# Four edits at the seams between the stages of a two-layer encoder trunk: a shorter wait, a split in halves, another order on VectorE and GpSimd, and other load times

## The chip, the cores and the metric

The kernel runs on one core of a Trainium2 chip. The metric is the device time of one execution in microseconds (us), the median of several executions.

## The reference

A trunk of two layers over 1024 tokens of width 1024, batch 1, all in float32. What is computed, cut to the matrices:

```python
cond = silu(c)
for i in range(2):
    shift1, scale1, gate1, shift2, scale2, gate2 = split(cond @ mod_w[i] + mod_b[i], 6)
    h = rms_norm(x, norm1_gain[i]) * (1 + scale1) + shift1
    if i == 0:
        y = swa_sink_attention(h, ...)        # q, k, v of width 1024, 128, 128; window of 128 keys; @ w_o
    else:
        uv = gelu(h @ w_uv)                   # 1024 x 4096
        u, v = split(uv, 2)
        v = layer_norm(v, v_gain)
        s = einsum('gij,bnjgc->bnigc', masked(w_s), blocks(v)) + s_bias
        y = (u * s) @ w_o                     # 2048 x 1024
    x = x + gate1 * y
    h = rms_norm(x, norm2_gain[i]) * (1 + scale2) + shift2
    x = x + gate2 * (square(relu(h @ w1)) @ w2)     # 1024 x 4096, 4096 x 1024
```

## The kernel before

**Numbers.** Each float32 product is made of three matmuls: both operands are split into a high part (an `ACT.Copy` into fp32r on ScalarE, `split_hi` and `weight_high`) and a low part (source minus high part, on GpSimd or VectorE), and high x high, low x high and high x low are added up in PSUM. A weight block is 1024 x 128 (`w_raw`, `w_hi`, `w_lo`, two slots of 128 x 1024).

**Three products in the fast form.** `fast_mlp(L)` runs three times: for the MLP of layer 0 (L.layer 0), for the gated stage of layer 1 (1, `L.gated`), for the MLP of layer 1 (2). The first product (up) has 16 pairs of output blocks. Pairs 0 and 1 are *plain*: 8 k-steps of 3 matmuls for each of two blocks and two halves of the tokens. The other 14 (n = 0 to 13 in the code, output pair j = n + 2) are Strassen-like: 7 products (t = 0 to 6) of 12 matmuls of 128 x 512 each. The second product (down) follows with pairs n = 14 and up, in couples that alternate on TensorE: (14, t), (15, t), (14, t + 1) and so on. A combination of weight quarters (`S_1` to `S_4`, GpSimd, line 853) is the weight of products 1 to 4. Its low part is made on GpSimd for t < 3 (line 858) and on VectorE for t >= 3 (line 1831).

**Outputs of the first product.** For each pair the ReLU and square of four blocks (B12, B22, B11, B21; `squared`, line 1836) and four differences of them (T3, T1, T2, T4; `output_diff`, line 1840) are made on VectorE and stored to `hid_dram` by SyncE's queue, one DMA each (line 642). The second product reads them back by operand, four pairs in one load of 1 MB on ScalarE's queue (`load_operand`, line 1143); then `operand_high` (ScalarE, 128 x 2048, line 1139) and `operand_low` (VectorE, 128 x 2048, line 1825).

**SyncE's queue is a fixed list.** At the start of `load_fast` the order is: the four plain blocks, the quarters of n = 0, `save_pair(0)`, `load_early(1)` (A11 and A21 of n = 1), `save_pair(1)`, and only then, in the loop, `load_a12(1)`, `load_a22(1)`, `load_early(2)`, `save_pair(2)`. `save_pair(j)` waits for each of the seven blocks of pair j in turn; the last is T4. The change does not touch this list. `S_1` of a pair needs its A21 and A22, `S_2` needs `S_1`, and the low part of product t = 1 follows `S_2` in GpSimd's list.

**The end of a stage.** Layers 0 and 1 of `fast_mlp` keep the last four output pairs' operands for a plain `closing` (TensorE line 2212, matmuls counted under line 2180): 4 pairs of blocks on the first half of the tokens, then 4 on the second. Its units alternate between the PSUM tiles pp[0] and pp[1]. The last couple before it writes pp[0] and pp[2] (first of the couple) and pp[3] and pp[2] (second). VectorE adds each down product to x (line 1935, counter `x_ev`).

**The start of a stage.** `opening_pair` runs plain pair 0 into pp[3] and pp[0] while VectorE and ScalarE normalise; then `plain_unit` twice. The weight split of plain pair 1, block 0, needs slot 0, which pair 0, block 0 frees three k-steps before TensorE has finished pair 0. VectorE's list there: `combine_inputs` (lines 1800 to 1817), the outputs of pair 0, `operand_low` of inputs 1, 2, 4, 6, two weight lows, the outputs of pair 1, then `up_step(0)`. ScalarE copies product t = 2 of n = 0 into a tile (line 1340) that the ReLU of pair 1 uses, so it waits for the last square of pair 1 (`u_quad`), and TensorE's t = 4 waits for that copy.

Of the kernel before, what the change touches and what calls it, by code (L numbers as in the profile page):

```python
# [15 lines left out]
KC = D // P  # L16
HALF = 512
# [80 lines left out]
def build(nc, x_in, c_in, pos_in, weights, mod_w, cols, mats, ws_in, bias_in, q_dram, v_dram, out):  # L98
# [5 lines left out]
    with ctx:  # L104
# [125 lines left out]
        v_pad = sem("v_pad")  # L230
        quad_in = [sem(f"quad_in{i}") for i in range(QUADS)]
# [119 lines left out]
        class Layer:  # L351
# [430 lines left out]
        def _(pool):  # L782
# [25 lines left out]
            def fast_weights(L):  # L808
# [94 lines left out]
        def _(act):  # L903
# [215 lines left out]
            def fast_mlp(L):  # L1119
# [166 lines left out]
                first = L.first  # L1286
                act.wait_ge(gemm, 2 * first + 1)
                split_hi(first + 1, 0)
# [38 lines left out]
                for p in range(PRODUCTS * L.pairs):  # L1327
# [13 lines left out]
                    if last and t % 2 == 0:  # L1341
# [70 lines left out]
        def _(dve):  # L1412
# [382 lines left out]
            def fast_mlp(L):  # L1795
# [59 lines left out]
                def plain_outputs(j, tiles, by):  # L1855

                    if j:
                        dve.wait_ge(hid_out, L.stored(j))
# [3 lines left out]
                    squared(j, O_B11, tiles[0][:, 0:HALF], by[0][:, 0:HALF])  # L1862
                    dve.wait_ge(u_quad, L.quad(j, 2))
                    output_diff(j, O_T3, O_B22, O_B12)
                    late_diffs(j)
                    squared(j, O_B21, tiles[1][:, 0:HALF], by[1][:, 0:HALF])
                    last_diff(j)

                def up_step(n):
# [10 lines left out]
                    for t in range(POOL_LOWS + (2 if n == 0 else 0), PRODUCTS):  # L1880
                        weight_low(n, t)
                    dve.wait_ge(f_copy, L.threes + 3 * n + 3)
                    add(3, banks[1], banks[1], 2)
                    if last:
# [3 lines left out]
                        operand_low(1)  # L1888
                        return
# [3 lines left out]
                    add(4, copied[1], banks[0], 1)  # L1893
# [33 lines left out]
                def down_step(n, t):  # L1927
# [12 lines left out]
                    if L.couple(n) == 0:  # L1940
                        if L.second(n) and t < 5:
                            operand_low(t + 2)
# [179 lines left out]
                else:  # L2122
                    plain_outputs(0, (pp[3], pp[0]), (tmp[:, 0, :], tmp[:, 1, :]))
                operand_low(1)
                dve.wait_ge(t_sum, L.sums + 13)
                operand_low(2)
                if L.gated:
                    stats(2)
                    stats(3)
                for t in (4, 6):  # L2130
                    operand_low(t)
# [518 lines left out]
```

## Time and profile before

| | us |
|---|---|
| median of 3 runs (lowest 2188.77, highest 2193.66) | 2189.37 |
| the profiled execution's own time | 2189.19 |
| its span in the profile | 2187.4 |
| TensorE matmuls busy | 2112.1 (97%) |
| VectorE busy | 1515.4 (69%) |
| ScalarE busy | 934.7 (43%) |
| GpSimd busy | 946.5 (43%) |

The profile's span runs from the first to the last instruction; 1.8 us lie around it. "Idle before" is the time an engine stood still ahead of an instruction, with the engine and line that released it. PEclk or "granted clock" is the share of TensorE's full clock: 1.00 is 2.4 GHz and 0.50 is 1.2 GHz.

### The profile page before, as it was taken

How to read it: one execution, taken by the hardware profiler on the slowest of the kernel's cores; microseconds unless marked ns; L12 is line 12 of the kernel's file. 1: busy time of each engine (PE TensorE's matmuls, PEld its weight loads, DVE VectorE, ACT ScalarE, POOL GpSimd, SP SyncE). 2: the span in 40 equal slices, each digit the busy share in tenths (PEclk: the TensorE clock that was granted, in tenths of full speed). 3: DMA queues.
4: the chain of work that ended last, by engine and by line, in shares of the span. 5: the costliest groups of instructions: out<-in, count | busy, mean ns of one | idle time of the engine just before them, and what ended most of it. 6: DMA issues, size and time to landing. Idle time of an engine off the chain costs nothing. (4 is left out here: it accounts for less than half of the span.)

```text
span 2187.4 us, 27285 instructions
## 1 busy us (share of the span) xinstructions
PE 2112.1 (97%) x9700; PEld 1714.5 (78%) x9700; DVE 1515.4 (69%) x1775; ACT 934.7 (43%) x1453; POOL 946.5 (43%) x600
## 2 busy tenths in 40 slices
PE   6999999999999999999899999999999999999999
PEld 4886687788887888787777788778778888778887
DVE  8679689766537878567787554756786666865673
ACT  4337543433344442334444666533343434443341
POOL 0124412555547466312443333622165555664753
PEclk8999999999999999999999999999999999999999
DMA  7363532444445664331665455633244444655352
GB/s 273 117 182 97 204 114 73 158 155 154 145 164 166 214 230 157 98 96 61 191 211 184 153 183 173 190 127 95 68 145 154 159 155 172 212 178 172 98 180 90
DMA packets 188896, 336.30 MB, mean 154 GB/s; under 512 B 32737, under 2 KB 55137, under 8 KB 188258
## 3 DMA queue, kind: packets, MB, share of 16 engines
q1 hardware_dynamic: 130018, 216.15, 29.8%
q10 hardware_dynamic: 58752, 118.50, 16.1%
q8 instruction: 75, 1.23, 0.2%
q14 instruction: 51, 0.42, 0.1%
HBM read 249.65 MB, written 83.89 MB: 152 GB/s over the span
## 5 line engine op out<-in xcount | busy, mean ns | idle before, releaser
L2541 PE MATMUL pp<-hid_lo,w_hi 128*128 128x512 f32 x1184 | 468.8, 396 | 16.6 <-POOL w_lo L858 8.4
L2541 PE MATMUL pp<-hid_lo,w_lo 128*128 128x512 f32 x1184 | 462.7, 391 | 0.0
L2541 PE MATMUL pp<-hid_hi,w_hi 128*128 128x512 f32 x1184 | 462.5, 391 | 0.0
L1133 ACT ACTIVATE w_hi<-mod_t 128x512 fp32r<-128x512 f32 x296 | 186.7, 631 | 426.8 <-POOL mod_t L853 225.8
L2541 PE MATMUL pp<-h_hi,w_hi 128*128 128x512 f32 x888 | 349.2, 393 | 2.6 <-issue 2.6
L2541 PE MATMUL pp<-h_hi,w_lo 128*128 128x512 f32 x888 | 346.2, 390 | 0.0
L2541 PE MATMUL pp<-h_lo,w_hi 128*128 128x512 f32 x888 | 346.2, 390 | 0.0
L785 POOL TENSOR_TENSOR w_lo<-w_raw,w_hi 128x1024 fp32r<-128x1024 f32 x44 | 112.6, 2560 | 479.1 <-ACT w_hi L908 479.1
L2180 PE MATMUL pp<-h_hi,w_hi 128*128 128x512 f32 x736 | 274.8, 402 | 24.0 <-POOL w_lo L785 10.0
L858 POOL TENSOR_TENSOR w_lo<-w_raw,w_hi 128x512 fp32r<-128x512 f32 x58 | 84.4, 1455 | 466.6 <-ACT w_hi L1133 420.0
L2541 PEld LDWEIGHTS pp<-hid_lo,w_hi 128*128 128x128 f32 x1184 | 223.6, 189 | 70.7 <-POOL w_lo L858 14.5
L2180 PE MATMUL pp<-h_lo,w_hi 128*128 128x512 f32 x736 | 268.9, 394 | 0.0
L2180 PE MATMUL pp<-h_hi,w_lo 128*128 128x512 f32 x736 | 268.8, 394 | 0.0
L1935 DVE SCALAR_TENSOR_TENSOR x<-pp,mod,x 128x512 f32<-128x512 f32 x224 | 166.6, 746 | 141.8 <-PE pp L2541 141.6
L2541 PEld LDWEIGHTS pp<-hid_lo,w_lo 128*128 128x128 f32 x1184 | 223.1, 188 | 47.7
L2541 PEld LDWEIGHTS pp<-hid_hi,w_hi 128*128 128x128 f32 x1184 | 223.6, 189 | 44.5
L858 POOL TENSOR_TENSOR w_lo<-mod_t,w_hi 128x512 fp32r<-128x512 f32 x148 | 239.1, 1615 | 13.4 <-ACT w_hi L1133 13.4
L853 POOL TENSOR_TENSOR mod_t<-w_raw 128x512 f32<-128x512 f32 x116 | 159.3, 1373 | 191.6 <-DVE w_lo L1831 161.4
L2541 PEld LDWEIGHTS pp<-h_hi,w_hi 128*128 128x128 f32 x888 | 167.2, 188 | 37.8 <-issue 4.0
L2541 PEld LDWEIGHTS pp<-h_hi,w_lo 128*128 128x128 f32 x888 | 167.0, 188 | 35.3
L2541 PEld LDWEIGHTS pp<-h_lo,w_hi 128*128 128x128 f32 x888 | 167.2, 188 | 33.6
L2180 PEld LDWEIGHTS pp<-h_hi,w_hi 128*128 128x128 f32 x736 | 138.5, 191 | 61.9 <-issue 13.1
(227 smaller groups left out, 3186.5 us busy)
## 6 DMA issues: line engine op xcount, KB each, us to landing
wide_f<-hid_dram ACTq DMA_DIRECT2D x64, 1024.0 KB, 5.8
hid_dram<-wide_f SPq DMA_DIRECT2D x247, 256.0 KB, 3.1
w_raw<-weights SPq DMA_DIRECT2D x232, 256.0 KB, 3.1
w_raw<-weights SPq DMA_DIRECT2D x70, 512.0 KB, 3.5
wide_f<-weights SPq DMA_DIRECT2D x64, 256.0 KB, 4.5
wide_f<-mod_w ACTq DMA_DIRECT2D x48, 256.0 KB, 3.9
mod_first<-mod_w SPq DMA_DIRECT2D x16, 512.0 KB, 15.3
mod_t<-mod_w ACTq DMA_DIRECT2D x16, 512.0 KB, 4.4
```

Of the source, the lines that this page charges most:

```text
L785: nc.gpsimd.tensor_tensor(out=w_lo[:, s, :, :], in0=w_raw[:, s, :, :], in1=w_hi[:, s, :, :].bitcast(f32), op=ALU.subtract).then_inc(lo_don ...
L853: nc.gpsimd.tensor_tensor(out=out, in0=in0, in1=in1, op=op).then_inc(w_sum, 1)
L858: nc.gpsimd.tensor_tensor(out=L.weight_quad(w_lo, n, t), in0=L.weight_source(n, t), in1=L.weight_quad(w_hi, n, t).bitcast(f32), op=ALU.sub ...
L1133: nc.scalar.activation(L.weight_quad(w_hi, n, t), L.weight_source(n, t), ACT.Copy).then_inc(w_high, 1)
L1935: V.scalar_tensor_tensor(out=xn, in0=L.product_banks(n)[BANK[t]], scalar=mod[:, L.gate, 2 * q + m:2 * q + m + 1], in1=xn, op0=ALU.mult, op ...
L2180: last = T.matmul((pp[s] if tile is None else tile)[:, cs], w[:, s, order[k] if order else k, :], r[:, k, cs], start=(k == 0 and w is w_hi ...
L2541: last = T.matmul(bank, w[:, i, :], r[:, i, :], start=(t in FRESH and i == 0 and w is high and r is hi), stop=(i == QUADS - 1 and w is low ...
```

## The change

Four places of `fast_mlp` and its neighbours:

1. TensorE's wait ahead of `closing` asks for the last update of the first pair of the last couple, not of the second. In `closing` the first unit runs its 8 k-steps in a row and then the second unit; before, the eighth k-step of the first came after four of the second.
2. Plain pair 1, block 0: ScalarE and GpSimd split the block in two halves of 4 k-steps (128 x 512), with two new semaphores, and TensorE starts after the first half.
3. VectorE's list at the start of the two ungated stages (`plain_start`): all four squares of a pair come before its differences; `operand_low(6)` and the differences of pair 1 come later (T3 after all weight lows of n = 0; T1, T2, T4 in `up_step(0)` behind the sum of product t = 4).
4. First operands of the second product: `load_operand(0, t)` is issued at every product t = 0 to 6 of the last up pair (before: 0 to 3 at t = 0, 2, 4, 6 and 4 to 6 in the first down pair); the high part of operand 2 and its low part move ahead of the down product; in the first couple GpSimd makes `S_1` and `S_2` of the first pair before the low part of the second pair's product 0.

```diff
             def sums_done(self, n, r):
+                if self.couple(n) == 0 and r in (S_1, S_2):
+                    return 4 * (self.pairs_before + FAST_UP) + 2 * self.second(n) + (1 if r == S_1 else 2)
 # GpSimd, fast_weights
-                for pair in range(1, PLAIN_PAIRS):
-                    for s in range(2):
-                        split_lo(L.first + pair, s)
+                pool.wait_ge(half_high, L.layer + 1)
+                second_low(0).then_inc(half_low, 1)
+                pool.wait_ge(hi_done, 2 * L.first + 3)
+                second_low(1).then_inc(lo_done, 1)
+                split_lo(L.first + 1, 1)
...
-                    for n in (first, first + 1):
-                        weight_low(n, 0)
-                        if c:
-                            sum_of(n, S_1)
-                    if c == 0:
-                        sum_of(first, S_1)
-                        sum_of(first + 1, S_1)
-                    for r, t in ((S_2, 1), (S_4, 2)):
-                        for n in (first, first + 1):
-                            sum_of(n, r)
-                            weight_low(n, t)
+                    weight_low(first, 0)
+                    sum_of(first, S_1)
+                    if c == 0:
+                        sum_of(first, S_2)
+                    weight_low(first + 1, 0)
+                    sum_of(first + 1, S_1)
+                    if c:
+                        sum_of(first, S_2)
+                    weight_low(first, 1)
+                    sum_of(first + 1, S_2)
+                    weight_low(first + 1, 1)
+                    for n in (first, first + 1):
+                        sum_of(n, S_4)
+                        weight_low(n, 2)
 # ScalarE
-                split_hi(first + 1, 0)
+                for part, counter in ((0, half_high), (1, hi_done)):
+                    ks = slice(QUADS * part, QUADS * part + QUADS)
+                    nc.scalar.activation(w_hi[:, 0, ks, :], w_raw[:, 0, ks, :], ACT.Copy).then_inc(counter, 1)
...
-                    if last and t % 2 == 0:
+                    if last:
                         act.wait_ge(f_mm, L.mms + p + 1)
                         if t == 0:
                             act.wait_ge(hid_out, L.stored(L.first_out + QUADS))
-                        load_operand(0, t // 2)
-                    if n == FAST_UP and t < 3:
-                        load_operand(0, t + 4)
+                        load_operand(0, t)
...
-                    if last and t in (3, 5):
-                        group_operand(0, t // 2 - 1)
-                    if n == FAST_UP and t < 5:
-                        group_operand(0, t + 2)
+                    if last and 3 <= t < 6:
+                        group_operand(0, t - 3)
+                    if n == FAST_UP and t < 4:
+                        group_operand(0, t + 3)
 # VectorE
+                def plain_start():
+                    plain_squares(0, (pp[3], pp[0]), (tmp[:, 0, :], tmp[:, 1, :]))
+                    plain_diffs(0)
+                    operand_low(1)
+                    dve.wait_ge(t_sum, L.sums + 13)
+                    operand_low(2)
+                    operand_low(4)
+                    weight_low(0, 3)
+                    dve.wait_ge(hid_out, L.stored(1))
+                    plain_squares(1, (pp[1], pp[2]), (tmp[:, 0, :], mod_acc[:, :]))
+                    weight_low(0, 4)
+                    weight_low(0, 5)
+                    weight_low(0, 6)
+                    dve.wait_ge(u_quad, L.quad(1, 2))
+                    output_diff(1, O_T3, O_B22, O_B12)
+                    operand_low(6)
...
+                    if n == 0:                      # up_step, behind add(3, ...)
+                        add(4, copied[1], banks[0], 1)
+                        late_diffs(1)
+                        last_diff(1)
...
 # TensorE
-                    for k in range(KC - 1):
+                    for k in range(KC):
                         if k % QUADS == 0:
                             pe.wait_ge(op_low, quads + k // QUADS)
-                        products(0, k, hi, lo, (0,), order=order)
-                    ready(pair0, 1)
-                    for k in range(4):
-                        products(1, k, hi, lo, (0,), order=order)
-                    products(0, KC - 1, hi, lo, (0,), order=order).then_inc(gemm, 1)
-                    for k in range(4, KC):
-                        last = products(1, k, hi, lo, (0,), order=order)
+                        last = products(0, k, hi, lo, (0,), order=order)
                     last.then_inc(gemm, 1)
+                    unit(pair0, 1, hi, lo, halves=(0,), order=order)
...
-            pe.wait_ge(x_ev, fast[0].updates(fast[0].pairs - 1, 6))
+            pe.wait_ge(x_ev, fast[0].updates(fast[0].pairs - 2, 6))
             closing(fast[0].first + PLAIN_PAIRS, h_hi, h_lo, 2, quads=fast[0].lows_ready(DOWN_GROUPS[0], 0))
             fast_mlp(fast[1])
-            pe.wait_ge(x_ev, fast[1].updates(fast[1].pairs - 1, 6))
+            pe.wait_ge(x_ev, fast[1].updates(fast[1].pairs - 2, 6))
```

## Rows read from the trace of the kernel before

**Rows 1.** The page: busy time of each engine, share of the span, instructions.
```profile
PE 2112.1 (97%) x9700; PEld 1714.5 (78%) x9700; DVE 1515.4 (69%) x1775; ACT 934.7 (43%) x1453; POOL 946.5 (43%) x600
```

**Rows 2.** Waits of TensorE, whole span: total us, times, longest.
```profile
PE pp L2180 <- POOL w_lo L785: 10.0, 7, 3.2
```

**Rows 3.** Timeline of TensorE, first closing: start, us, [idle before].
```profile
894.52 0.50 PE L2180 MATMUL pp<-h_hi,w_hi 128*128 128x512 f32 x1 [2.28 <-DVE x L1935]
908.23 0.50 PE L2180 MATMUL pp<-h_hi,w_hi 128*128 128x512 f32 x1 [0.88 <-POOL w_lo L785]
```

**Rows 4.** Timelines of VectorE and GpSimd, first closing.
```profile
891.51 2.29 DVE L1970 TENSOR_TENSOR h_lo<-wide_f,h_hi 128x2048 fp32r<-128x2048 f32 x1 [0.75 <-ACT h_hi L1157]
...
895.17 5.23 DVE L1970 TENSOR_TENSOR h_lo<-wide_f,h_hi 128x2048 fp32r<-128x2048 f32 x2 [0.70 <-ACT h_hi L1157]
...
905.80 2.37 POOL L785 TENSOR_TENSOR w_lo<-w_raw,w_hi 128x1024 fp32r<-128x1024 f32 x1 [9.75 <-ACT w_hi L908]
```

**Rows 5.** Stretches: TensorE, its loads, VectorE, ScalarE, GpSimd busy; clock; DMA.
```profile
361.00:366.00 5.00, 5.00 (x12) 3.86 (x13) 5.00 (x6) 0.48 (x1) 2.39 (x1) 0.50 0.56 197
896.00:899.00 3.00, 3.00 (x9) 2.32 (x8) 3.00 (x2) 0.94 (x1) 0.06 (x1) 0.51 0.48 164
1613.00:1619.00 6.00, 5.68 (x24) 4.43 (x24) 3.15 (x6) 1.58 (x3) 1.28 (x1) 1.00 0.73 237
```

**Rows 6.** Timelines, start of the first MLP.
```profile
355.00 1.06 ACT L908 ACTIVATE w_hi<-w_raw 128x1024 fp32r<-128x1024 f32 x1 [2.30 <-PE pp L2180]
...
360.76 1.19 PE L2180 MATMUL pp<-h_hi,w_hi 128*128 128x512 f32 x2 [3.17 <-POOL w_lo L785]
...
379.50 3.72 ACT L1139 ACTIVATE hid_lo<-wide_f 128x2048 fp32r<-128x2048 f32 x2 [0.44 <-DMA hid_dram<-wide_f]
...
391.62 0.50 PE L2541 MATMUL pp<-hid_lo,w_hi 128*128 128x512 f32 x1 [0.71 <-POOL w_lo L858]
397.88 0.47 PE L2541 MATMUL pp<-hid_lo,w_hi 128*128 128x512 f32 x1 [0.53 <-ACT tmp L1340]
```

**Rows 7.** Timelines, from the last difference of pair 1 to product (1, 1), first MLP.
```profile
397.08 0.69 DVE L1840 TENSOR_TENSOR wide_f<-wide_f 128x512 f32<-128x512 f32 x1
398.49 0.42 SPq L593 DMA_DIRECT2D w_raw<-weights  x1
402.47 1.64 POOL L853 TENSOR_TENSOR mod_t<-w_raw 128x512 f32<-128x512 f32 x1 [2.31 <-issue]
405.78 1.30 POOL L858 TENSOR_TENSOR w_lo<-mod_t,w_hi 128x512 fp32r<-128x512 f32 x1
408.88 0.39 PE L2541 MATMUL pp<-hid_lo,w_hi 128*128 128x512 f32 x1
```

**Rows 8.** Timeline of TensorE, start of the gated stage and of the third.
```profile
1013.18 0.70 PE L2180 MATMUL pp<-h_hi,w_hi 128*128 128x512 f32 x2 [1.43 <-POOL w_lo L785]
...
1613.08 0.47 PE L2541 MATMUL pp<-hid_lo,w_hi 128*128 128x512 f32 x1 [2.67 <-ACT tmp L1340]
1624.60 0.39 PE L2541 MATMUL pp<-hid_lo,w_hi 128*128 128x512 f32 x1
```

**Rows 9.** Timelines, first couple of the first MLP's second product.
```profile
651.71 0.63 ACT L1133 ACTIVATE w_hi<-wide_f 128x512 fp32r<-128x512 f32 x1 [3.50 <-DMA wide_f<-weights]
652.42 1.28 POOL L858 TENSOR_TENSOR w_lo<-wide_f,w_hi 128x512 fp32r<-128x512 f32 x1 [4.63 <-ACT w_hi L1133]
...
660.99 0.47 PE L2541 MATMUL pp<-hid_lo,w_hi 128*128 128x512 f32 x1 [1.71 <-DVE hid_hi L1825]
663.21 3.34 POOL L853 TENSOR_TENSOR mod_t<-w_raw,mod_t 128x512 f32<-128x512 f32 x1
667.84 0.50 PE L2541 MATMUL pp<-hid_lo,w_hi 128*128 128x512 f32 x1 [1.12 <-POOL w_lo L858]
674.71 0.47 PE L2541 MATMUL pp<-h_hi,w_hi 128*128 128x512 f32 x1 [0.88 <-issue]
```

**Rows 10.** The page, DMA issues: count, KB each, median us from issue to landing.
```profile
wide_f<-hid_dram ACTq DMA_DIRECT2D x64, 1024.0 KB, 5.8
```

More of the change, by code:

```diff
@@ L230, in build @@
         v_pad = sem("v_pad")
+        half_high, half_low = sem("half_high"), sem("half_low")
         quad_in = [sem(f"quad_in{i}") for i in range(QUADS)]
@@ L859, in weight_low, with second_low @@
                                             in1=L.weight_quad(w_hi, n, t).bitcast(f32), op=ALU.subtract).then_inc(w_low_p, 1)
-                for pair in range(1, PLAIN_PAIRS):
-                    for s in range(2):
-                        split_lo(L.first + pair, s)
+                def second_low(part):
+                    ks = slice(QUADS * part, QUADS * part + QUADS)
+                    return nc.gpsimd.tensor_tensor(out=w_lo[:, 0, ks, :], in0=w_raw[:, 0, ks, :],
+                                                   in1=w_hi[:, 0, ks, :].bitcast(f32), op=ALU.subtract)
+                pool.wait_ge(half_high, L.layer + 1)
[3 more added lines that the diff above has]
+                split_lo(L.first + 1, 1)
                 for n in range(FAST_UP):
@@ L1286, in fast_mlp @@
                 first = L.first
+                act.wait_ge(raw_in[0], 16 * (first + 1) + 16)
                 act.wait_ge(gemm, 2 * first + 1)
-                split_hi(first + 1, 0)
+                for part, counter in ((0, half_high), (1, hi_done)):
+                    ks = slice(QUADS * part, QUADS * part + QUADS)
+                    nc.scalar.activation(w_hi[:, 0, ks, :], w_raw[:, 0, ks, :], ACT.Copy).then_inc(counter, 1)
                 if L.gated:
@@ L1853, in last_diff, with plain_squares @@
                     output_diff(j, O_T4, O_B21, O_T2)
-                def plain_outputs(j, tiles, by):
-                    if j:
-                        dve.wait_ge(hid_out, L.stored(j))
+                def plain_squares(j, tiles, by):
                     dve.wait_ge(f_relu, L.relus + 2 * j + 2)
@@ L1862, in plain_outputs, with plain_diffs @@
                     squared(j, O_B11, tiles[0][:, 0:HALF], by[0][:, 0:HALF])
+                    squared(j, O_B21, tiles[1][:, 0:HALF], by[1][:, 0:HALF])
+                def plain_diffs(j):
                     dve.wait_ge(u_quad, L.quad(j, 2))
@@ L1865, in plain_outputs @@
                     late_diffs(j)
-                    squared(j, O_B21, tiles[1][:, 0:HALF], by[1][:, 0:HALF])
                     last_diff(j)
+                def plain_start():
[14 more added lines that the diff above has]
+                    operand_low(6)
                 def up_step(n):
@@ L1879, in up_step @@
                     last = n == FAST_UP - 1
-                    for t in range(POOL_LOWS + (2 if n == 0 else 0), PRODUCTS):
-                        weight_low(n, t)
+                    if n:
+                        for t in range(POOL_LOWS, PRODUCTS):
+                            weight_low(n, t)
                     dve.wait_ge(f_copy, L.threes + 3 * n + 3)
@@ L1888, in up_step @@
                         operand_low(1)
+                        operand_low(2)
                         return
+                    if n == 0:
+                        add(4, copied[1], banks[0], 1)
+                        late_diffs(1)
+                        last_diff(1)
                     dve.wait_ge(hid_out, L.stored(j))
@@ L1892, in up_step @@
                     squared(j, O_B12, banks[1], rectified[0])
-                    add(4, copied[1], banks[0], 1)
+                    if n:
+                        add(4, copied[1], banks[0], 1)
                     dve.wait_ge(f_sum, L.threes + 3 * n + 2)
@@ L1940, in down_step @@
                     if L.couple(n) == 0:
-                        if L.second(n) and t < 5:
-                            operand_low(t + 2)
+                        if L.second(n) and t < 4:
+                            operand_low(t + 3)
                         if not L.gated and not L.second(n) and 1 <= t <= 4:
@@ L2121, in fast_mlp @@
                     stats(1)
[L2122 to L2127, printed above, removed]
+                    operand_low(1)
+                    dve.wait_ge(t_sum, L.sums + 13)
+                    operand_low(2)
                     stats(2)
                     stats(3)
-                for t in (4, 6):
-                    operand_low(t)
-                weight_low(0, 3)
-                weight_low(0, 4)
-                if not L.gated:
-                    plain_outputs(1, (pp[1], pp[2]), (tmp[:, 0, :], mod_acc[:, :]))
+                    for t in (4, 6):
+                        operand_low(t)
+                    weight_low(0, 3)
+                    weight_low(0, 4)
+                else:
+                    plain_start()
                 if L.closes:
@@ L2150, in fast_mlp @@
                     gate_slot(FAST_UP, 0)
+                    operand_low(2)
                 for p in range(PRODUCTS * FAST_UP, PRODUCTS * L.pairs):
@@ L2488, in plain_unit @@
                 def plain_unit(pair, s, tile, turns=()):
-                    pe.wait_ge(lo_done, 2 * pair + s + 1)
+                    if s == 0:
+                        pe.wait_ge(half_low, L.layer + 1)
+                    else:
+                        pe.wait_ge(lo_done, 2 * pair + s + 1)
                     for k in range(KC):
+                        if (s, k) == (0, QUADS):
+                            pe.wait_ge(lo_done, 2 * pair + 1)
                         last = products(s, k, h_hi, h_lo, tile=tile)
```

## The prediction, on record before the changed kernel was run

> **What bounds the kernel.** First the page: TensorE's matmuls are busy 97% of the span [rows 1], so time can only come out of its idle gaps or of its slow clock. Then the list of who TensorE waited for: the largest release is the low half of plain weights, 10.0 us in 7 waits [rows 2]. Then TensorE's timeline, to see where each gap lies; and the table of stretches, because a gap can cost twice. In rows 5 the granted clock is 0.50 (1.2 GHz) for five microseconds after the 3.17 us gap of [rows 6], and 0.51 in the stretch behind the 2.28 us gap of a closing, while no drop follows the 2.67 us gap of the third stage [rows 5, 8]. Last, the timelines of the other engines around each gap, to see what becomes late when the gap closes. The four products of 12 matmuls between 397.88 and 408.88 [rows 6, 7] take 11.0 us with one restart in them; I count 2.72 us for an unhindered product, 10.9 us for 48 matmuls, 21.8 us for the 96 of two plain blocks.
>
> **Part 1, the closings (two of them).** TensorE stands 2.28 us, until VectorE has made the last update, which stands in its list behind a 128 x 2048 subtraction that ends at 893.80 [rows 3, 4]. The first unit writes pp[0]; the second pair of the couple used pp[3], so the shorter wait is already met when TensorE arrives at 894.52 - 2.28 = 892.24. The next waits: k-step 4 needs that subtraction (893.80) at 892.24 + 2.72 = 894.96, met. 48 matmuls then end at 903.1. The next unit began at 908.23 after 0.88 us of idle, because `gemm` of the first unit came late (its last k-step was put after four others) and ScalarE's 1.06 us and GpSimd's 2.37 us follow it [rows 3, 4, 6]. With the new order `gemm` comes at 897.7, the low half is ready by 898.9, or, since VectorE's two subtractions hold GpSimd up until 900.40 [rows 4], by 902.8. VectorE must still clear a tile and make one update behind 900.40, about 903.3. So the unit starts at about 903.3 instead of 908.23: 4.9 us, of which 2.28 and 0.88 are idle and the rest is the slow clock that followed the gap. Bounds: 4.0 if that update waits for GpSimd's low, 5.1 if nothing does. The second closing shows the same gaps of 2.28 and 0.88. Two closings: 9.8 us.
>
> **Part 2, halves.** At the start of the first MLP the halves of ScalarE (about 0.6 us for 128 x 512, from half of 1.06) and GpSimd (1.30, [rows 7]) end at about 357.1, before TensorE has finished pair 0 at 360.76 - 3.17 = 357.59 [rows 6]. The idle of 3.17 goes, and with it the stretch at 0.50: between 361 and 366 it cost half of 5 us, 2.5 us. In the gated stage the gap is 1.43 [rows 8], in the third the same within 0.02, without a drop. The second half has 5.4 us of cover (4 k-steps of 6 matmuls). ScalarE and GpSimd pay one more instruction each, hidden. So TensorE comes to product (0, 0) earlier by 5.7, 1.4 and 1.4 us. What that is worth is read from what follows.
>
> **Part 3, squares first, in stages 0 and 2.** At the start of the first MLP the gaps 0.71 and 0.53 remain [rows 6], in the third 2.67 [rows 8]. The order removes the 2.67 (ScalarE's copy then waits for four squares of pair 1, not for three differences and `operand_low(6)` too). But two things come late. First, ScalarE: its two high parts of 3.72 us in all can't start before the stores of pair 0 have landed (379.50, [rows 6]); behind them lie 1.0 for a ReLU, two weight highs of 0.63, 1.0 for a ReLU and 0.6 for the copy, 387.1 to 387.8. So product (0, 2), for which TensorE is there at 357.6 + 21.8 + 2 x 2.72 = 384.8, starts at about 387.9, (0, 4) at 393.3. Second, SyncE's list. T4 of pair 1 is now made behind the sum of product t = 4. Not before 393.3 + 2.8 (the product) + 0.7 (the sum) + 2.0 (three differences at 0.69) = 398.8, I take 399.2; before it ended at 397.77 [rows 7]. `load_a22(1)` stands behind it in SyncE's list. From T4's end to the end of the low part of (1, 1) the trace has 407.08 - 397.77 = 9.3 us, made of the store's issue, the loads, their landing (GpSimd stood until 402.47), two sums and the low part [rows 7]. So (1, 1) starts at about 408.6 and not, as free running would have it, at 357.6 + 21.8 + 8 x 2.72 = 401.1. Before it was 408.88 [rows 7]: all of the 5.7 + 0.71 + 0.53 us come back as one idle of about 4.4 us, 0.3 are left. And an idle of that size is longer than the 3.17 that brought the slow clock, so I take 2.3 us for that (between the 1.7 of a closing and 2.5). If the 3.1 us ahead of (0, 2) brings a drop too, 2.5 more; I count 0.5 of it. First MLP: 0.3 - 2.3 - 0.5 = -2.5 us, a loss. Bounds: -6 and +7.8 (free running).
> Third stage, the same working: (0, 2) at 1603.8, (0, 4) at 1609.2, T4 at 1615.7, + 9.4 = 1625.1 against 1624.60 [rows 8]: -0.5, and -2.3 for the clock: -2.8 us. Bounds -6 and +4.6. The gated stage has its own list, without this order; I keep 1.0 of its 1.43.
>
> **Part 4, the second product.** At its start stand 1.71, 1.12 and 0.88 us in the first MLP [rows 9], the same three within 0.04 in the third stage; the gated one has only two such gaps, 2.1 in all. The operands come one product earlier each, so the 1.71 and the 0.88 go. The 1.12 is GpSimd's chain: nine instructions from 652.42 to 667.8, where TensorE is released. Two now come earlier, so seven remain behind 652.5, each 1.3, and each held for 2.05 us more when it meets a 128 x 2048 subtraction (3.34 against 1.30, [rows 9, 7]). With two held the low part that (14, 2) needs comes at 666.1, TensorE is there at 664.7. Of 4.9 (the three gaps, a smaller one of about 0.3 between them and restarts) I take off 1.4 there and 0.7 for what this pushes: 2.8 us each for the first and third, and 1.3 for the gated one: 6.9 us. Bounds per stage 0 and 4.9 (all gaps).
> The Trainium skill, SBUF — State Buffer, "Who interferes with whom", says that a VectorE instruction with two SBUF inputs and a GpSimd one that reads SBUF exclude each other for a whole instruction. The 3.34 against 1.30 agrees. By that rule the third early subtraction (operand 2) holds GpSimd a third time, 668.1 instead of 666.1, no gain at (14, 2), and the sum for this part would be 3.9 and not 6.9. I keep two, because ScalarE's highs space the subtractions out.
>
> **Sum.** 9.8 - 2.5 - 2.8 + 1.0 + 6.9 = 12.4 us from 2189.19 (the profiled execution's time; the median of the runs is 0.18 above), 2176.8; I say 2177.
>
> **Rivals.** (a) *All gaps close:* T4 of pair 1 does not hold the reload, or holds it behind other cover. Speaks for it: VectorE has its weight lows out of the way. Against: SyncE's list [rows 7]. Gain 9.8 + 7.8 + 4.6 + 1.4 + up to 6.9 = 30, 2159 to 2165. (b) *The stage starts lose less:* the later idle brings no slow clock, as after the 2.67, or the reload lands sooner: 4 to 9 us better than my sum, 2167 to 2172. (c) *The early loads crowd:* seven loads of 1 MB in seven products are 385 GB/s, where a load that takes 5.8 us [rows 10] had two products to itself; part 4's gain is lost and the stage starts stay: 2183 to 2188, near no change. (d) *Slower:* the same crowding at the same place makes the weights of pair 15 late. Before, ScalarE waited for them until 651.71 [rows 9]; with a high of 0.63 and a low of 1.28 behind it, and TensorE there at 661 - 1.7 - 2.7 = 656.6, they may be 3 us later before TensorE stands. Behind that each us costs one, and from about 3 us of idle 2.6 more by clock. It decides from landings near 658: 3 x (2.3 + 3 + 2.6) = 24 us against a sum of 12.4, about 2200.
>
> **Chances.** Forecast 0.54, (a) 0.12, (b) 0.16, (c) 0.13, (d) 0.05. The forecast's own range is 2172 to 2183; with (b) and most of (c) 2167 to 2185, which leaves out (a), (d) and the edges. A change of 0.2%, 4.4 us, is about what a measurement of this kernel can tell from none. Faster by more 0.84, within 0.11, slower 0.05.
>
> **What would show it.** Right: no idle ahead of the closings' first matmul, clock 1.00 there; no idle at the first plain block of pair 1; a new gap of 4 us or more before product (1, 1) of the first and third stage, released by GpSimd, whose sum waits for a DMA, and clock 0.50 behind it; (14, 2) idle about 1 us. Wrong: no such gap, or the loads of w_raw issued before T4, or a gap ahead of (15, 0).

## The result, and the profile after

The changed kernel takes 2195.04 us (median of 8 runs, 2192.53 to 2196.72); the kernel before, beside it, 2190.66 (8 runs). The ratio is 1.0025, 95% interval 1.0015 to 1.0035: slower by 4.4 us in the medians and 5.5 by the ratio, where 12.4 us faster were forecast. The profiled execution of after took 2192.53 us (span 2190.7), against 2189.19 before: +3.3 us.

The two closings did what they should, and something else lost more than both gave. To find it I lay the matmuls of the fast products of the two traces side by side (6216 in each, in the same order) and take how much later each product starts in the changed kernel. The difference of that shift over a stretch is what the stretch lost (+) or won. "Couple" is the first couple of the second product, pairs 14 and 15. The halves of the first MLP lie in the first row, those of the two other stages in the closing rows: product (0, 0) is the first one behind them.

| stretch | forecast | measured in after |
|---|---|---|
| first MLP, up to product (2, 0) | +2.5 | +3.7 |
| first MLP, couple | -2.8 | +1.5 |
| closing 1, and halves of the gated stage | -4.9 - 1.0 | -7.0 |
| gated stage, couple | -1.3 | **+8.1** |
| closing 2, and halves of the third stage | -4.9 - 1.4 | -7.0 |
| third stage, (0, 0) to (2, 0) | +4.2 | +3.6 |
| third stage, couple | -2.8 | +0.8 |
| all the rest | 0 | -0.3 |

A closing alone is 5.3 (experiment 1), so 1.7 of each closing row are halves. The third stage's start, halves included, is 3.6 - 1.7 = +1.9, against 4.2 - 1.4 = +2.8 forecast.

Timeline of TensorE after (start, us, instruction, [idle before <- releaser]), the gaps that answer to [rows 6 to 9], and the one of the gated stage:
```profile
389.21 0.47 PE L2580 MATMUL pp<-hid_lo,w_hi 128*128 128x512 f32 x1 [3.91 <-ACT tmp L1357]
410.84 0.76 PE L2580 MATMUL pp<-hid_lo,w_hi 128*128 128x512 f32 x1 [3.43 <-POOL w_lo L861]
664.93 0.50 PE L2580 MATMUL pp<-hid_lo,w_hi 128*128 128x512 f32 x1 [1.52 <-POOL w_lo L861]
669.46 0.50 PE L2580 MATMUL pp<-hid_lo,w_hi 128*128 128x512 f32 x1 [1.51 <-POOL w_lo L861]
673.98 0.50 PE L2580 MATMUL pp<-hid_lo,w_hi 128*128 128x512 f32 x1 [1.51 <-POOL w_lo L861]
1382.11 2.08 PE L2519 MATMUL pp<-ws,mod_acc 128*128 128x128 f32 x8 [7.71 <-ACT mod_acc L1243]
```
Gone are the 3.17 us ahead of pair 1, and the 2.28 and 0.88 of the closings. New are 3.91 and 3.43 in the first MLP, and 1.95 and 3.51 at the same two places of the third stage. In the first MLP's couple, 1.71 + 1.12 + 0.88 became three times 1.5. And in the gated stage, behind the last product of its last up pair, TensorE stands for 7.7 us, at a place where the kernel before had no gap at all.

The stretches around them (us of the stretch, then busy us and count of TensorE, its weight loads, VectorE, ScalarE, GpSimd; granted clock; DMA share; GB/s): one behind the 3.43, one at the closing, then the gated stage:
```profile
411.00:413.00 2.00, 2.00 (x5) 1.62 (x6) 1.93 (x3) 0.94 (x2) 2.00 (x2) 0.50 0.91 329
896.00:900.00 4.00, 4.00 (x19) 3.34 (x18) 2.97 (x3) 3.20 (x3) 1.33 (x1) 1.00 0.13 52
...
1360.00:1365.00 5.00, 5.00 (x31) 4.40 (x30) 1.83 (x3) 1.96 (x6) 0.00 (x0) 1.00 1.02 389
1365.00:1370.00 5.00, 5.00 (x25) 4.17 (x25) 2.95 (x5) 4.40 (x7) 1.30 (x1) 1.00 1.08 358
1370.00:1375.00 5.00, 4.40 (x24) 3.46 (x22) 1.72 (x1) 0.00 (x0) 2.58 (x2) 1.00 1.07 363
1375.00:1380.00 5.00, 0.00 (x0) 0.00 (x0) 0.00 (x0) 0.63 (x2) 0.00 (x0) 0.69 1.06 323
1380.00:1385.00 5.00, 2.89 (x11) 2.70 (x12) 2.41 (x3) 5.00 (x8) 3.04 (x3) 0.50 0.83 284
```
At the closing the clock stays at 1.00 (in [rows 5] it was 0.51 there). In the gated stage a stretch comes in which no engine does anything to speak of while the DMA engines are full: TensorE 0.00, VectorE 0.00, ScalarE 0.63, GpSimd 0.00, DMA share 1.06 at 323 GB/s. The whole core waits for the weights of pair 15. ScalarE's and SyncE's timelines name it:
```profile
1355.46 0.40 ACTq L1157 DMA_DIRECT2D wide_f<-hid_dram  x1
...
1358.12 0.38 ACTq L1157 DMA_DIRECT2D wide_f<-hid_dram  x1
...
1360.85 0.37 ACTq L1157 DMA_DIRECT2D wide_f<-hid_dram  x1
...
1364.46 0.37 ACTq L1157 DMA_DIRECT2D wide_f<-hid_dram  x1
...
1368.09 0.37 ACTq L1157 DMA_DIRECT2D wide_f<-hid_dram  x1
1379.37 0.63 ACT L1147 ACTIVATE w_hi<-wide_f 128x512 fp32r<-128x512 f32 x1 [9.97 <-DMA wide_f<-weights]
...
1380.42 1.63 ACT L1243 ACTIVATE mod_acc<-mod_acc,vscale 128x128 f32<-128x128 f32 x4
```
```profile
1363.31 8.18 SPq L596 DMA_DIRECT2D wide_f<-weights  x4
```
Five loads of 1 MB are issued in 12.6 us. Behind the third of them SyncE comes to its four weight loads of pair 15 (256 KB each), and takes 8.18 us for their issue alone; the next two of 1 MB fall beside it. The list of DMA issues in this stretch gives their time to landing (KB each, median us):
```profile
wide_f<-hid_dram ACTq DMA_DIRECT2D x7, 1024.0 KB, 9.9
hid_dram<-wide_f SPq DMA_DIRECT2D x8, 256.0 KB, 5.1
w_raw<-weights SPq DMA_DIRECT2D x5, 256.0 KB, 3.4
wide_f<-weights SPq DMA_DIRECT2D x4, 256.0 KB, 14.0
```
14.0 us for the weights; in the same stretch of the kernel before it is 6.4. ScalarE stands 9.97 us for the first high part of pair 15. Queued behind that in ScalarE's list is the scaling of the gated stage's normalised v (`v_dram`), L1243, at 1380.42, and it is this that TensorE's matmuls at 1382.11 wait for: not for pair 15's weights themselves. Behind the gap the granted clock is 0.50 (1.2 GHz), and TensorE's matmuls take 0.63 us instead of 0.39 until some 1387.

### The profile page after: what moved, and what is told of

It reads as the page before. It is cut to its first block and busy times, and to the rows that moved or that the text cites. A ratio compares the mean times of both kernels' runs of the same rounds, so it can differ in the third digit from the quotient of the medians.

```text
span 2190.7 us, 27291 instructions
## 1 busy us (share of the span) xinstructions
PE 2109.8 (96%) x9700; PEld 1714.5 (78%) x9700; DVE 1508.7 (69%) x1775; ACT 934.6 (43%) x1456; POOL 943.1 (43%) x603
## 5 line engine op out<-in xcount | busy, mean ns | idle before, releaser
L861 POOL TENSOR_TENSOR w_lo<-mod_t,w_hi 128x512 fp32r<-128x512 f32 x148 | 234.5, 1584 | 27.1 <-ACT w_hi L1147 27.1
L788 POOL TENSOR_TENSOR w_lo<-w_raw,w_hi 128x1024 fp32r<-128x1024 f32 x41 | 107.2, 2616 | 268.5 <-ACT w_hi L922 268.4
L2580 PEld LDWEIGHTS pp<-h_hi,w_hi 128*128 128x128 f32 x888 | 167.3, 188 | 35.6 <-DVE w_lo L1846 0.7
L1147 ACT ACTIVATE w_hi<-w_raw 128x512 fp32r<-128x512 f32 x174 | 109.3, 628 | 155.6 <-PE pp L2580 145.8
```

Of the source, the lines that this page charges most:

```text
L788: nc.gpsimd.tensor_tensor(out=w_lo[:, s, :, :], in0=w_raw[:, s, :, :], in1=w_hi[:, s, :, :].bitcast(f32), op=ALU.subtract).then_inc(lo_don ...
L861: nc.gpsimd.tensor_tensor(out=L.weight_quad(w_lo, n, t), in0=L.weight_source(n, t), in1=L.weight_quad(w_hi, n, t).bitcast(f32), op=ALU.sub ...
L1147: nc.scalar.activation(L.weight_quad(w_hi, n, t), L.weight_source(n, t), ACT.Copy).then_inc(w_high, 1)
L2580: last = T.matmul(bank, w[:, i, :], r[:, i, :], start=(t in FRESH and i == 0 and w is high and r is hi), stop=(i == QUADS - 1 and w is low ...
```

## The experiments

Ten kernels. Times are against the runs of the kernel before taken beside them (medians 2189.2 to 2190.0; beside the changed kernel it was 2190.66, so a difference from the changed kernel may be 1 us off). Kernels 9 and 10 ran on another chip than 1 to 8, each beside the kernel before. The table at the end of this section has their stretches.

**1. The closings alone.** The kernel before, with this part of the change:
```diff
-                    for k in range(KC - 1):
+                    for k in range(KC):
...
-                    products(0, KC - 1, hi, lo, (0,), order=order).then_inc(gemm, 1)
...
+                    unit(pair0, 1, hi, lo, halves=(0,), order=order)
...
-            pe.wait_ge(x_ev, fast[0].updates(fast[0].pairs - 1, 6))
+            pe.wait_ge(x_ev, fast[0].updates(fast[0].pairs - 2, 6))
```


> The kernel before with the closings' part alone. The two closings in the changed kernel's trace each took back 5.2 to 5.5 us. If that gain belongs to the closings, this kernel is 10 to 11 us faster than before (ratio 0.995). If part of it was only the recovery of time that the changed kernel had lost just ahead of them, it is 8 us or less.

Measured: 2179.08 us (5 runs), ratio 0.9954 (0.9942 to 0.9967), 10 us faster. Each closing gives 5.3 us here, as in the changed kernel. The gain is theirs, and it is there whatever stands ahead. The stretches of this kernel, at the first closing:
```profile
890.00:894.00 4.00, 4.00 (x20) 3.30 (x19) 3.25 (x3) 3.20 (x3) 1.00 (x1) 1.00 0.17 67
894.00:898.00 4.00, 4.00 (x19) 3.31 (x18) 3.29 (x3) 3.23 (x3) 1.66 (x1) 1.00 0.24 70
```
TensorE is busy throughout at clock 1.00: the gaps of [rows 3] and the slow stretch of [rows 5] are gone together.

**2. The changed kernel without part 4.** Loads, high and low parts of the second product's operands and GpSimd's list are those of before; the rest is the change.

> The changed kernel with part 4 undone (loads, high and low parts of the second product's operands and GpSimd's list as before). Theory: part 4 cost about 10 us, nearly all in the gated stage, where the weights of pair 15 landed 6.5 us later behind early loads of 1 MB; so this kernel is 5 to 9 us faster than before, about 10 faster than the changed one, and has no idle near 7 us ahead of the last pair of the gated stage. Rival: the loss comes from the starts of the stages (halves and squares), and part 4 is near nothing: then it stays within 3 us of the changed kernel.

Measured: 2185.32 us (11 runs), 0.9981 (0.9972 to 0.9990): 4 us faster than before, 9.7 below the changed kernel. The 7.7 us are gone, and the gated couple costs 1.3 instead of 8.1. The gain against before is a little below the 5 to 9 expected, and why is not shown: the trace is of this kernel's slowest execution (2188.38), which has +6.5 at the third stage's start where the changed kernel, with the same code there, had +3.6.

**3. Only the loads as before.** All is as in the changed kernel but the place of the seven issues:
```diff
-                    if last:
+                    if last and t % 2 == 0:
...
-                        load_operand(0, t)
+                        load_operand(0, t // 2)
+                    if n == FAST_UP and t < 3:
+                        load_operand(0, t + 4)
```


> The changed kernel in which only the issue of the second product's seven 1 MB loads is as before (every second product of the last pair, the last three in the next pair); the order of highs, subtractions and GpSimd's list is the new one. Theory, early loads crowd SyncE's four 256 KB weight loads: the weights of pair 15 land some 6 us earlier in the gated stage, its 7.7 us idle goes, the time is 8 to 10 us below the changed kernel's. Rival, the new order of GpSimd's and VectorE's lists costs it: 2 us or less below the changed kernel's.

Measured: 2185.75 us (12 runs), 0.9984 (0.9975 to 0.9993), 9.3 below the changed kernel. This separates the transfers from the order of the lists: the order is still the new one, and the loss of the gated couple is 0.6 (the trace is of the fastest execution, 2181.59). The weights of pair 15 land in 7.3 us and not in 14.0. The same list of issues, of this kernel:
```profile
wide_f<-hid_dram ACTq DMA_DIRECT2D x7, 1024.0 KB, 7.2
...
wide_f<-weights SPq DMA_DIRECT2D x4, 256.0 KB, 7.3
```
ScalarE's wait for them (timeline) falls from 9.97 to 2.26 us:
```profile
1367.32 0.63 ACT L1147 ACTIVATE w_hi<-wide_f 128x512 fp32r<-128x512 f32 x1 [2.26 <-DMA wide_f<-weights]
```
In the first and third stage the couple costs 0.1 and -0.1: with the old loads the new order of high parts, subtractions and sums is worth nothing; the 6.9 us forecast had counted on order and early loads together. The gaps only move. In the first MLP one of 2.51 us, again behind GpSimd's low part, takes the place of the three:
```profile
665.80 0.50 PE L2582 MATMUL pp<-hid_lo,w_hi 128*128 128x512 f32 x1 [2.51 <-POOL w_lo L861]
```

**4. The reload ahead of the last stores.** The changed kernel, in which SyncE issues the reload of two quarters after three stores of pair 1 (B22, T3, B11) and not after all seven:
```diff
-                    save_pair(1)
+                    save_pair(1, slice(0, 3))
+                    load_a12(1)
+                    load_a22(1)
+                    save_pair(1, slice(3, None))
                 for n in range(FAST_UP):
-                    load_a12(n + 1)
-                    load_a22(n + 1)
+                    if n or L.gated:
+                        load_a12(n + 1)
+                        load_a22(n + 1)
```


> The changed kernel, but in the first MLP and the third stage SyncE issues the reload of A12 and A22 ahead of the last four stores of pair 1 (T1, T2, B21, T4). Theory, the reload stands behind T4: the 3.43 and 3.51 us idle ahead of product (1, 1) and the slow clock behind go, 4 to 9 us below the changed kernel's time. Rival, the reload is not what (1, 1) waits for, or its cover goes at once to the next wait (ScalarE's copies, the last differences): less than 2 us below, with the idle moved to (1, 2) or later.

Measured: 2186.72 us (11 runs), 0.9986 (0.9977 to 0.9995), 8.3 below the changed kernel. The start of the first MLP costs -0.1 instead of +3.7, that of the third stage 0.0 instead of +3.6. SyncE's timeline shows why, the reload at 396.54 where after had it at 402.74:
```profile
396.01 0.43 SPq L645 DMA_DIRECT2D hid_dram<-wide_f  x1
396.54 0.89 SPq L596 DMA_DIRECT2D w_raw<-weights  x2
400.23 2.74 SPq L645 DMA_DIRECT2D hid_dram<-wide_f  x4
```
The cover behind it is thin: one product later TensorE stands again, for ScalarE's copy, as the rival had it, only for less than half as long:
```profile
411.40 0.47 PE L2584 MATMUL pp<-hid_lo,w_hi 128*128 128x512 f32 x1 [1.64 <-ACT tmp L1361]
```

**5. Three loads early, four late.** The changed kernel; loads 0, 1 and 2 stay early, 3 goes behind product 6, 4 to 6 into the next pair:
```diff
-                    if last:
+                    if last and t in (0, 1, 2, 6):
...
-                        load_operand(0, t)
+                        load_operand(0, min(t, 3))
+                    if n == FAST_UP and t < 3:
+                        load_operand(0, t + 4)
```


> The changed kernel, with loads 0, 1 and 2 of the second product's operands issued early, behind products 0, 1 and 2 of the last pair; load 3 behind its product 6 and loads 4 to 6 in the next pair, both as in the kernel before. Theory, bytes crowd: the four 256 KB weight loads of pair 15 go out near products 4 and 5, now free of 1 MB loads, so the gated stage's 7.7 us idle goes: 6 to 9 us below the changed kernel's time. Rival, any early load behind product 1 delays the last stores or the chain behind them: less than 3 us below.

Measured: 2187.50 us (12 runs), 0.9994 (0.9983 to 1.0004), 7.5 below the changed kernel. The gated couple costs 1.5, the weights land in 8.7 us. So it is not that an early load delays things as such: the two loads (3 and 4) issued at 1364 and 1368, beside the weights, decide (load 3 goes out at 1375 here, 4 to 6 later still). The same stretches as above, in this kernel:
```profile
1365.00:1370.00 5.00, 5.00 (x28) 4.29 (x27) 2.92 (x5) 4.57 (x7) 1.30 (x1) 1.00 1.08 363
1370.00:1375.00 5.00, 4.97 (x26) 3.91 (x25) 2.54 (x2) 1.68 (x4) 3.03 (x3) 1.00 1.11 292
```
The DMA share reaches 1.11, as full as in the changed kernel, and TensorE is still busy in 5.00 and 4.97 of 5 us: a full row of DMA engines says nothing by itself. What counts is how many bytes share the engines with those that are waited for.

**6. The squares alone.** The kernel before with part 3 alone.

> The kernel before with part 3 alone (squares ahead of differences, T4 of pair 1 behind the sum of product 4), in the first MLP and the third stage. Theory: T4 of pair 1 comes later, the reload behind it in SyncE's list as well, and (1, 1) waits: 2 to 6 us slower than before (each stage loses 1 to 3). Rival: without the halves TensorE comes 1.7 to 5.7 us later to (0, 0), so T4 is in time and the gaps of 0.71, 0.53 and 2.67 close: 2 to 4 us faster.

Measured: 2193.97 us (12 runs), 1.0022 (1.0012 to 1.0031), 4.7 slower. The two starts lose 4.0 and 2.6 us, 6.6 together. TensorE stands ahead of (1, 1) in both, though it comes there without the halves' 5.7 us:
```profile
410.65 0.79 PE L2563 MATMUL pp<-hid_lo,w_hi 128*128 128x512 f32 x1 [4.25 <-POOL w_lo L858]
...
1626.09 0.50 PE L2563 MATMUL pp<-hid_lo,w_hi 128*128 128x512 f32 x1 [3.77 <-POOL w_lo L858]
```

**7. Closings and halves.** The kernel before with parts 1 and 2. The halves are this (TensorE's side):
```diff
-                    pe.wait_ge(lo_done, 2 * pair + s + 1)
+                    if s == 0:
+                        pe.wait_ge(half_low, L.layer + 1)
+                    else:
+                        pe.wait_ge(lo_done, 2 * pair + s + 1)
                     for k in range(KC):
+                        if (s, k) == (0, QUADS):
+                            pe.wait_ge(lo_done, 2 * pair + 1)
```


> The kernel before with the closings and the halves. The closings alone gave 10 us. Theory, the time won ahead of (0, 0) in the first MLP and the third stage is given back at the next waits (stores, ScalarE's copies, reload), and only the gated stage keeps its 1.7: 11 to 13 us faster than before. Rival, the halves are worth their idle and clock in all three stages (5.7 + 1.7 + 1.7): 17 to 19 us faster.

Measured: 2177.57 us (6 runs), 0.9938 (0.9921 to 0.9955), 11.7 us faster than before by the medians and 13.6 by the ratio, and with kernel 8 the fastest of all; that it beats kernel 1 is likely but inside the intervals. In the first MLP the 6.0 us won ahead of (0, 0) come back at (0, 2), where ScalarE's copies and GpSimd's low part stand behind the stores of pair 0:
```profile
389.84 0.80 PE L2553 MATMUL pp<-hid_lo,w_hi 128*128 128x512 f32 x1 [4.63 <-POOL w_lo L859]
```

**8. All but part 4, with the reload first.** The kernel before with closings, halves and squares, and the edit of kernel 4.

> The kernel before with closings, halves and squares, and the reload of A12 and A22 ahead of the last four stores of pair 1; part 4 left out. If part 4 (10 us) and the place of the reload (8 us) add, it is 16 to 20 below the changed kernel's time, 11 to 15 faster than before. If both took back the same time twice, it is no more than 12 below the changed kernel's, 7 faster than before.

Measured: 2177.47 us (5 runs), 0.9947 (0.9930 to 0.9963): 17.6 below the changed kernel, 11.8 faster than before. The two repairs add (9.7 and 8.3). It also shows that part 3, mended, is worth nothing beyond kernel 7: the gaps it closes, 0.71, 0.53 and 2.67, come back at the next wait.

**9. Part 4 alone,** on the kernel before.

> The kernel before with part 4 alone. Theory: the early 1 MB loads make the weights of pair 15 late in the gated stage whatever the starts of the stages do: 8 to 11 us slower than before, 7 to 9 of it there, under 2 in each of the others. Rival: the delay needs the other parts (GpSimd's and VectorE's lists shifted by halves and squares): 3 us slower or less.

Measured: 2197.58 us (8 runs), 1.0033 (1.0021 to 1.0044), 7.6 slower; by the interval 4.6 to 9.6. The couples lose 1.1, 8.4 and 0.8 us, 10.3 together; the pairs of the gated stage ahead of its couple are 5.1 us faster in this trace, in which the change has no part (see below). TensorE's wait is the same, so it needs neither halves nor squares:
```profile
1381.55 2.08 PE L2490 MATMUL pp<-ws,mod_acc 128*128 128x128 f32 x8 [7.93 <-ACT mod_acc L1234]
```

**10. Part 4 with GpSimd's old list.** As 9, without this part:
```diff
-                    for n in (first, first + 1):
-                        weight_low(n, 0)
-                        if c:
-                            sum_of(n, S_1)
+                    weight_low(first, 0)
+                    sum_of(first, S_1)
...
+                        sum_of(first, S_2)
+                    weight_low(first + 1, 0)
+                    sum_of(first + 1, S_1)
```


> The kernel before with part 4's loads, highs and subtractions, but GpSimd's list (sums and low parts of pairs 14 and 15) as it was. Theory: the loads cost it, so within 2 us of part 4 alone, 7 to 11 us slower than before. Rival: GpSimd's new list costs a share of 3 us or more, then this one is that much faster than part 4 alone.

Measured: 2205.44 us (6 runs), 1.0064 (1.0052 to 1.0076), 8 us slower still. Neither theory had this: GpSimd's new list costs nothing, it saves 8 us. In the old one the low part of (15, 0) stands ahead of pair 14's sums; when the loads make pair 15's weights late, all of pair 14's work waits behind it. In the first and the third stage:
```profile
665.78 0.80 PE L2541 MATMUL pp<-hid_lo,w_hi 128*128 128x512 f32 x1 [6.01 <-POOL w_lo L858]
...
1893.59 0.79 PE L2541 MATMUL pp<-hid_lo,w_hi 128*128 128x512 f32 x1 [5.83 <-POOL w_lo L858]
```
The three couples lose 4.3, 9.6 and 3.4 us here, against 1.1, 8.4 and 0.8 in kernel 9. So the change carries a remedy in the same part as the ailment. Against the old loads, in kernel 3, the remedy has nothing to cure.

**The stretches of all,** us of shift against the kernel before, worked out as in the section on the result:

| kernel | 1st start | 1st couple | closing 1, halves | gated, rest | gated couple | closing 2, halves | 3rd start | 3rd couple |
|---|---|---|---|---|---|---|---|---|
| changed | +3.7 | +1.5 | -7.0 | 0.0 | +8.1 | -7.0 | +3.6 | +0.8 |
| 1 closings | -0.4 | -0.1 | -5.3 | -2.7 | +0.6 | -5.3 | +1.1 | +0.2 |
| 2 no part 4 | +4.4 | -0.4 | -7.0 | +1.1 | +1.3 | -7.1 | +6.5 | +0.6 |
| 3 old loads | +4.0 | +0.1 | -7.1 | -2.9 | +0.6 | -7.1 | +5.1 | -0.1 |
| 4 reload first | -0.1 | +1.2 | -7.0 | +2.3 | +7.9 | -7.1 | 0.0 | +0.8 |
| 5 three early | +4.3 | +0.8 | -7.0 | +0.8 | +1.5 | -7.1 | +4.9 | -0.1 |
| 6 squares | +4.0 | +0.2 | 0.0 | -3.9 | +0.3 | 0.0 | +2.6 | +0.1 |
| 7 closings, halves | +0.1 | -0.1 | -6.0 | +0.8 | -0.3 | -7.0 | +0.7 | +0.3 |
| 8 all but 4, reload first | +0.2 | +0.6 | -7.1 | -2.1 | +0.4 | -7.1 | +1.8 | +0.9 |
| 9 part 4 | +1.3 | +1.1 | 0.0 | -5.1 | +8.4 | -0.2 | +0.1 | +0.8 |
| 10 part 4, old list | -0.2 | +4.3 | -1.5 | -0.4 | +9.6 | 0.0 | +1.1 | +3.4 |

The large entries of a column belong to the part that touches it, except in "gated, rest": there -5.1 to +2.3 us appear with no edit in the place. In the other columns -1.5 to +1.3 do (closing 1 of kernel 10, first start of kernel 9), and the third start is +3.6 to +6.5 in four kernels that have the same code there (changed, 2, 3, 5). One profile is uncertain by that much, which is why the verdicts go by medians; the couples' +0.8 in the third stage can't be told from none.

## Why the prediction was wrong, step by step

**Closings, right.** Forecast 4.9 each, measured 5.3 (kernel 1). The reading that the second pair's wait was never needed, that the drop of the clock goes with the gap, and that the 0.88 goes too, all held. The bound of 5.1 was passed by a little: no update waited for GpSimd. One number of the working was off without weight in the sum: by its own terms the low half was due at 901.1 (897.7 + 1.06 + 2.37), not at 898.9.

**Halves, right, and the first one partly by luck.** In the two later stages 1.7 us against 1.4 read from the gaps; no idle at the first plain block of pair 1. In the first MLP (0, 0) started 5.9 us earlier, 5.7 were forecast. But in kernels 1, 6, 9 and 10, which have no halves, it started 1.0 to 1.2 us earlier too: behind the same 3.17 us gap the slow clock lasted less long (0.98 from 364 to 366 in kernel 6, 0.50 in [rows 5]). So some 4.8 of the 5.9 are the halves', and the 2.5 for the clock was read from a long case.

**Squares first, right in mechanism and nearly in size.** Forecast +2.5 and +2.8, measured +3.7 and +1.9, 5.6 against 5.3 in sum. VectorE's differences up to T4, SyncE's reload, GpSimd's sum and low part, in their timelines:
```profile
399.90 2.21 DVE L1855 TENSOR_TENSOR wide_f<-wide_f 128x512 f32<-128x512 f32 x3
```
```profile
402.74 0.99 SPq L596 DMA_DIRECT2D w_raw<-weights  x2
```
```profile
406.62 1.28 POOL L856 TENSOR_TENSOR mod_t<-w_raw 128x512 f32<-128x512 f32 x1 [7.15 <-issue]
...
409.52 1.27 POOL L861 TENSOR_TENSOR w_lo<-mod_t,w_hi 128x512 fp32r<-128x512 f32 x1
```
T4 ends at 402.11, where I had 399.2; from there to the end of the low part 8.7 us pass, where I took 9.3 from [rows 7]. T4 is later because the stores of pair 0 landed later: ScalarE starts its high parts at 382.00, not at the 379.50 of [rows 6]. The sum had kept that landing where it was; kernel 7 (halves, old order) has 381.91, kernel 6 (squares) 380.72, and VectorE's four differences of pair 0 take 5.78 us in the changed kernel, 5.74 in kernel 7 and 4.67 in kernel 6, against 3.28 before. So (0, 2) starts at 389.21 and not at 387.9, and the clock falls there, of which I had counted a fifth. Kernel 4 takes away T4's hold on the reload and nothing else, and both losses go: this step is shown. What the working did not draw from it: SyncE's order was the cheap thing to mend, worth 8 us.

**Part 4, the step that failed.** Forecast: "so the 1.71 and the 0.88 go", 2.8 us each in two stages and 1.3 in the gated one, -6.9. Measured 1.5 + 8.1 + 0.8, +10.4. It was two mistakes.

The larger: the gated stage was costed at its gaps alone. The crowding of rival (d) was what happened, but I had asked about it only in the first MLP, at pair 15's own weights. There its threshold held: it "decides from landings near 658"; ScalarE's high part of (15, 0) came at 658.35 of which 3.7 are the shift of the whole, so at 654.6, and (15, 0) itself started 0.3 us late. In the gated stage the same high part stands in ScalarE's list ahead of the scaling of the value tiles, which TensorE needs before pair 14 begins, and not at pair 15; and the DMA engines there carry v_dram and stores of the pair as well. So the prediction's own sign of being wrong, a gap ahead of (15, 0), would not have found it either. Before the change the same stretch had a DMA share of 1.03 to 1.08, and ScalarE waited 1.90 us for these weights (stretches, ScalarE's timeline and the list of issues, kernel before):
```profile
1363.00:1368.00 5.00, 5.00 (x30) 4.35 (x29) 2.93 (x5) 2.32 (x6) 0.99 (x1) 1.00 1.03 359
1368.00:1373.00 5.00, 5.00 (x27) 4.22 (x26) 3.16 (x3) 3.10 (x6) 0.30 (x1) 1.00 1.08 308
...
1372.88 0.63 ACT L1133 ACTIVATE w_hi<-wide_f 128x512 fp32r<-128x512 f32 x1 [1.90 <-DMA wide_f<-weights]
...
wide_f<-weights SPq DMA_DIRECT2D x4, 256.0 KB, 6.4
```
Those were the rows to look up: a transfer already waited for, on full engines, has no cover. Kernels 3 and 5 show the cause, 9 that it needs no other part of the change.

The smaller: in the two other stages the gaps were read as three gaps of their own, two of which earlier operands would close. The profile of before had named three releasers for them (VectorE, GpSimd, issue [rows 9]). In the changed kernel GpSimd releases all three, as one chain. Its timeline, after:
```profile
659.06 1.29 POOL L861 TENSOR_TENSOR w_lo<-wide_f,w_hi 128x512 fp32r<-128x512 f32 x1 [0.75 <-ACT w_hi L1147]
660.31 1.30 POOL L856 TENSOR_TENSOR mod_t<-wide_f 128x512 f32<-128x512 f32 x1
661.87 3.01 POOL L861 TENSOR_TENSOR w_lo<-mod_t,w_hi 128x512 fp32r<-128x512 f32 x1 [0.26 <-ACT w_hi L1147]
664.84 3.34 POOL L856 TENSOR_TENSOR mod_t<-mod_t,wide_f 128x512 f32<-128x512 f32 x1
668.14 1.26 POOL L861 TENSOR_TENSOR w_lo<-mod_t,w_hi 128x512 fp32r<-128x512 f32 x1
669.37 3.33 POOL L856 TENSOR_TENSOR mod_t<-w_raw,mod_t 128x512 f32<-128x512 f32 x1
672.66 1.27 POOL L861 TENSOR_TENSOR w_lo<-mod_t,w_hi 128x512 fp32r<-128x512 f32 x1
```
Seven instructions, as forecast, but three of them are held (3.01, 3.34, 3.33) where I kept two: 14.9 us from 659.06 to 673.93, against 13.6 in my sum. And the first begins 2.9 us later than before once the shift of 3.7 is taken off, since the weights land later here too. (14, 2) waits for its end. The exclusive lock that the Trainium skill states (SBUF — State Buffer, "Who interferes with whom") made the third hold, and the trace agrees with it, not with my reason against it (that ScalarE's highs space the subtractions out). Taking its side would have lowered part 4's gain to 3.9, and would not have found the gated stage.

**Sum.** -10.6 (closings) - 1.7 (gated halves) + 3.7 + 1.9 (starts) + 10.4 (part 4) - 0.3 = +3.4, the 3.3 of the profiled executions. Had part 4 been worth nothing, the forecast of the rest (-5.5) would have met kernel 2's -4.4.

**The rivals.** (a) and (b) did not happen. (c) was the case of the first and third stage, and (d) in the gated stage; a rival was counted either everywhere or nowhere, though the three stages share no list. Split by stage, (d) at the place with the least cover would have had far more than 0.05.

## What to carry to other kernels

When transfers are moved earlier, look up the smallest transfer that is already waited for in the same stretch, and how full the DMA engines are there; then follow what is queued behind its first reader, in each stage by itself, since the same edit meets another list in each. Several gaps in a row can be one chain even where the profile names a releaser of its own for each: follow each releaser back to what it waited for itself. An earlier operand then only moves them, and closes none. And a wait that is simply too strict, as those of the closings, is the gain that stays: its 5.3 us per place came in every kernel that had it, while what was won at the start of the first MLP was taken back at the next list in every kernel.

## What the runs showed of the hardware

- Four loads of 256 KB on SyncE's queue among 1 MB loads on ScalarE's queue: 14.0 us to landing (median; 9.9 for the 1 MB loads themselves) at a DMA share of 1.02 to 1.08 and 358 to 389 GB/s; with two of the big ones moved away 8.7, with the old places 7.3, and 6.4 in the kernel before. Their issue alone took 8.18 us (4.81 with the old places). The Trainium skill (Trainium Kernel Development and Optimization, Key Constraints) has it that DMAs of all queues run on the same 16 engines and interleave: the trace agrees, the small loads on a queue of their own landed no sooner than the big ones.
- The granted clock did not follow the length of a gap alone. It was 0.50 behind 3.43 us (start of the first MLP) and behind 7.71, and 0.51 behind the 2.28 of a closing [rows 5]. Behind the 2.51 of kernel 3 it fell as well (0.58 from 666.5 to 669.5), and behind 2.67 it stayed at 1.00 [rows 5, 8]. How it is decided the runs do not tell.
- The spread of "gated, rest", 7.4 us between profiles of kernels that have the same code there, was not expected, and its cause stays open.
